# ScalarE issues the weight transfers of the down projection from the third expert on

## What is computed

```
gu = t[tok] @ w_up[e] + b_up[e]                       # 1024 -> 2048
a  = minimum(gu[:, :1024], 7);  u = clip(gu[:, 1024:], -7, 7)
y  = ((u + 1) * a * sigmoid(1.702 * a)) @ w_down[e] + b_down[e]    # 1024 -> 1024
out[tok] += y * gate
```

## Time and profile before

| | us |
|---|---|
| median of 3 runs | 1723.51 |
| the three runs | 1723.09, 1723.51, 1733.51 |
| the profiled execution | 1729.49 |
| its span | 1727.8 |
| TensorE busy in the span | 1650.4 |
| VectorE, ScalarE, GpSimd busy | 522.4, 466.4, 194.3 |

### The profile page before, as it was taken

One profiled execution on the slowest core, in us unless ns is written; L12 is line 12 of the kernel. 1 busy time (PEld: TensorE's weight loads), 2 busy tenths in 40 slices (PEclk: granted clock), 3 DMA queues, 4 the chain that ended last, 5 costly groups with the idle time before them and its releaser, 6 DMA issues.

```text
span 1727.8 us, 44359 instructions
## 1 busy us (share of the span) xinstructions
PE 1650.4 (96%) x19448; PEld 1404.1 (81%) x19448; DVE 522.4 (30%) x1278; ACT 466.4 (27%) x930; POOL 194.3 (11%) x263
## 2 busy tenths in 40 slices
PE   7999999999999999998798999998999998999998
PEld 4899988798777778885445799996799996799996
DVE  6766785655356854000000000000100000000000
ACT  5245655533423432111101121111111111112111
POOL 0022000003331032100000000000000000000000
PEclk9999999999999999899999999999999999999999
DMA  5064232114437319899999999999999999999996
GB/s 227 22 216 119 85 124 100 48 62 134 134 104 268 108 56 386 294 383 400 411 407 401 410 401 402 411 399 389 404 400 407 404 409 389 402 406 398 398 405 241
DMA packets 99340, 499.59 MB, mean 289 GB/s; under 512 B 15198, under 2 KB 32694, under 8 KB 48496
## 3 DMA queue, kind: packets, MB, share of 16 engines
q1 hardware_dynamic: 84288, 458.39, 67.2%
q0 software_dynamic: 14768, 38.71, 8.2%
q10 hardware_dynamic: 144, 0.55, 0.1%
HBM read 485.61 MB, written 22.73 MB: 294 GB/s over the span
## 4 chain that ended last, share of the span: by engine, by line
PE 80%; DMA 11%; DVE 5%; issue 2%; SPq 1%; ACT 1%; POOL 0%; DVEq 0%; POOLq 0%; ACTq 0%
PE bank L1323 22%; PE bank L1321 13%; PE bank L1318 8%; DMA ring<-in_w_exp 8%; PE bank L805 7%; PE bank L705 5%; PE bank L860 5%; PE bank L732 3%; PE bank L1315 2%; PE bank L1124 2%; PE bank L1377 1%; PE bank L873 1%; DMA slab<-in_w_tok 1%; SPq L628 1%; PE bank L894 1%
## 5 line engine op out<-in xcount | busy, mean ns | idle before, releaser
L1323 PE MATMUL bank<-ring,slab 128*32 128x128 f32 x5760 | 644.2, 274 | 0.6 <-issue 0.6
L1321 PE MATMUL bank<-ring,slab 128*32 128x384 f32 x5760 | 636.6, 489 | 3.8 <-DMA ring<-in_w_exp 1.3
L1323 PEld LDWEIGHTS bank<-ring,slab 128*32 128x32 f32 x5760 | 626.0, 110 | 2.0 <-issue 1.3
L2604 DVE TENSOR_SCALAR slab<-bank 128x384 f32<-128x384 f32 (+2 forms) x64 | 33.1, 516 | 922.8 <-PE bank L1323 597.1
L1318 PE MATMUL bank<-ring,slab 128*64 128x256 f32 x2112 | 246.4, 387 | 26.5 <-DMA ring<-in_w_exp 26.0
L1318 PEld LDWEIGHTS bank<-ring,slab 128*64 128x64 f32 x2112 | 149.2, 139 | 113.4 <-DMA ring<-in_w_exp 36.3
L1321 PEld LDWEIGHTS bank<-ring,slab 128*32 128x32 f32 x5760 | 214.0, 109 | 12.2 <-issue 9.9
L1833 ACT ACTIVATE slab<-bank 128x384 f32<-128x384 f32 (+2 forms) x64 | 29.3, 458 | 444.8 <-PE bank L1323 292.8
L805 PE MATMUL bank<-ring_rounded 128*128 128x260 f32 x768 | 147.7, 291 | 0.0
L805 PEld LDWEIGHTS bank<-ring_rounded 128*128 128x128 f32 x768 | 117.8, 188 | 14.0 <-issue 11.9
L2744 POOL DMA_INDIRECT slab<-token_rows,small x31 | 31.1, 1002 | 575.5 <-PE bank L1310 529.9
(11 more groups left out here) (539 smaller groups left out, 2161.0 us busy)
## 6 DMA issues: line engine op xcount, KB each, us to landing
ring<-in_w_exp SPq DMA_DIRECT2D x384, 1024.0 KB
ring<-in_w_blk SPq DMA_DIRECT2D x40, 512.0 KB, 3.6
slab<-in_w_tok SPq DMA_DIRECT2D x4, 1304.0 KB
ring<-in_w SPq DMA_DIRECT2D x8, 512.0 KB, 3.5
ring<-in_w_out SPq DMA_DIRECT2D x2, 2048.0 KB, 14.7
xn<-in_xT SPq DMA_DIRECT2D x4, 520.0 KB
ring<-in_k_cmp SPq DMA_DIRECT2D x32, 64.0 KB, 3.6
ring<-in_k_cmp POOLq DMA_DIRECT2D x32, 64.0 KB, 2.7
```

Of the source, the lines that this page charges most:

```text
L1321: mm(bank[32 * g:32 * g + 32, c, 0:384], rows(32 * g, 32), w[:, 0:384], start=first, stop=last)
L1323: r = mm(bank[96:128, c, P * g:P * (g + 1)], rows(32 * g, 32), w[:, 384:512], start=first and g == 0, stop=last and g == 2)
```

## The change

ScalarE issues the four pieces of the down projection for blocks 2 to 31, at the start of its stream for the block, that is behind `scaled` of the block before. It loads the expert's number into a register of its own for that, and it waits once for `ovf_ready` ahead of the loop. SyncE issues only pieces 0 to 7 of these blocks. Blocks 0 and 1, the path for experts with more tokens than 128 (not taken with these inputs), the semaphores and the places in SBUF stay as they are.

```
@@ SyncE
             def expert(n, after):
                 e = expert_at(n)
-                for c, h in PIECE_ORDER:
+                for c, h in PIECE_ORDER[0:8]:
                     sp.wait_ge(S["half_used"], pieces_used(after, c, h))
                     expert_half(e, c, h)
@@ ScalarE
+            def down_weights(n):
+                e = act.value_load(order_row[0:1, n:n + 1], min_val=0, max_val=NE - 1)
+                for c, h in PIECE_ORDER[8:12]:
+                    act.wait_ge(S["half_used"], pieces_used(n - 1, c, h))
+                    act.dma_start(ring[:, half_of(c, h)], d["w_exp"][bass.ds((e * 6 + c) * P, P), h * HALF:(h + 1) * HALF])\
+                        .then_inc(piece_in[2 * c + h], 16)
...
             block_of(1, role_of(1), CAP[1], CAP[2])
+            act.wait_ge(S["ovf_ready"], 2)
             for n in range(2, NE):
+                down_weights(n)
                 block_of(n, role_of(n), CAP[n], CAP[n + 1] if n + 1 < NE else None)
```

## The result

| | before | after |
|---|---|---|
| median of the runs, us | 1723.51 | 1756.47 |
| lowest to highest | 1723.09 to 1733.51 | 1751.02 to 1759.89 |
| the profiled execution / its span | 1729.49 / 1727.8 | 1756.47 / 1754.8 |
| ratio, with 95% interval | | 1.0167 (1.0140 to 1.0194) |

The changed kernel is slower by 1.67%, 29 us (1.67% of 1724), 24 to 33 by the interval. The ratio is taken over all runs; the two medians alone lie 33.0 us apart, as one of the three runs before is 10 us above the others. The forecast was +24 and 1747.5, within 1727 to 1766.

The account below looks back on a forecast made before the run. Up to block 24's end piece delivery was taken to bound the kernel, afterwards TensorE's own work. Terms of 9 + 14 + 1 gave +24 us, taking the median from 1723.5 to 1747.5 us, range 1727 to 1766.

Parts of the forecast that it names:

- Up to the end of block 24 the time is the delivery of pieces: Whole kernel: piece delivery at 2.73 us each sets the time until block 24 ends, then TensorE's own work, untouched.
- SyncE and ScalarE at nothing: Issuing engines: SyncE's four dropped issues gain nothing; ScalarE's 2.5 us of new work per block fits in 2.94 us idle.
- (a): Ahead of block 2: down pieces issued 11 us later leave the transfer engines idle; +9 us, between 7 and 11.
- (b): Up to block 24's end: two queues alternate, so 5 more pieces are delivered before they are needed; +14 us.
- (c): Long MID blocks: with at most 8 pieces to run ahead, the transfer engines stand idle when all have landed; +1 us.
- MID blocks over 34.2: Sign against the prediction: MID blocks longer than 34.2 us, which no part of its sum holds.
- cross-check by blocks: Sum of expected changes in single blocks 2, 3, 5, 7, 8 and 16: +11 to +19 us.
- delivery account: Counts pieces delivered ahead by block 24's end: lead 5.5 where it was 0, costing 5 x 2.73 = 13.7 us.
- alternation case: Main case: the two hardware queues are served in turn; +24 us, own range 1741 to 1756, chance 0.62.
- Order of issue: Rival: transfers served in the order issued, so only the empty queue ahead of block 2 costs; +9 us, chance 0.15.
- Gaps filled by a second queue: Rival: two queues together move more per us in delivery-bound stretches; 1700 to 1722 us, chance 0.07.
- third rival: Worse than alternation: longer waits lower TensorE's clock in blocks 2, 3, 7, 16 and 24; +10 to +15 more, chance 0.11.

Follow-up runs that it names:

- late-issue run: Kernel before, SyncE issuing all pieces but holding the down pieces of blocks 2 to 31 until the whole block before has used its last piece: 4.7 us over before.
- two complementary sets of blocks: Changed kernel with ScalarE issuing down pieces only for MID blocks behind MID blocks, or only for all other blocks from 2 on: 14.8 and 30.0 us over before.
- 6 us of tiny packets: Kernel before, SyncE issuing all pieces, ScalarE adding the load, waits and four issues per block of 32 bytes a partition into unused columns: 6.2 us over before.
- load and waits alone: Kernel before, SyncE issuing all pieces, ScalarE adding the load of the expert's number and four waits per block, no issue: -1.6 us over before.
- run from block 3 on: Changed kernel, but SyncE issues all 12 pieces of block 2 and ScalarE begins with block 3: 24.3 us over before.
- alternation alone: Against the kernel before, ScalarE issues the next block's down pieces on its own queue as their places come free, within scaled: 15.3 us over before.
- repeated run: The changed kernel unaltered, run again beside the second group of experiments: 29.7 us over before.
- with the full clock: Changed kernel with 12 extra products of 128 columns ahead of three down pieces in blocks 2 to 5, 8, 16 and 24: 37.4 us over before.
- the 3.0 and 5.1 us of blocks 12 and 20: Changed kernel with ScalarE issuing down pieces only for blocks 12 to 14, 20 to 22 and 28 to 30: 5.5 us over before.

## Why the prediction was right

The class, the direction and the main mechanism were right: two queues served in turn, in a stretch bound by the delivery of pieces. That the total came so close owes something to luck. The runs show about 5 us for the term put at 9 and 15 for the one put at 14, and another 9 that appear only with both together and stand in no term.

*What bounds.* "Up to the end of block 24 the time is the delivery of pieces" held: 29.6 of the 30 us in the profile are there at that point. The late-issue run, the two complementary sets of blocks that don't add up, and the 6 us of tiny packets are what a full set of engines would show too.

*SyncE and ScalarE at nothing* held: ScalarE's issues ended 1.2 us before its next work (0.34 us each where 0.41 was taken), and load and waits alone measured -1.6 us (-4.1 to 1.0).

*(a) The dry queue ahead of block 2, +9* was mis-sized. The engines did idle 7.7 us there, but this term measured 4.7 alone (2.2 to 7.2) and 4.5 (28.8 less 24.3) as the difference of the run from block 3 on. Where the other 3 us come back was not found.

*(b) Pieces delivered early, +14* is the part that carried the forecast. The alternation is one to one (4.57 beside 4.19 MB), and alternation alone measured 15.3 (11.7 to 19.1). By the landings in the trace, five up pieces of block 25 had landed when block 24 ended at 1518.8 (the fifth just then; the fourth's landing isn't in the trace and is taken from its place in the queue), the number worked out before. The lengths of single blocks fared less well: at least 28 was said for blocks 2, 3 and 7 (25.7, 30.0, 27.7), about 30 for block 8 (30.4) and 29 for block 16 (30.8). Block 2 is short of it because its up pieces had landed before, so that ScalarE's first piece went alone. And the picture was half right: waits in the down stage were said, up by about 20. They are up by 16, and over half of them are for up pieces of the block itself, in block 3 all of them.

*(c) Idle engines, +1* was too small. The share is 0.94 in block 6 and 0.91 in block 7: 0.06 x 44.1 + 0.09 x 27.7 = 5 us, which the account for (b) had not covered, as it was worked out for block 24 alone. How much of it reaches the end no run tells.

*A term that was missing:* block 9, the first MID block, takes 39 us where it had taken 35.0. The prediction gave MID blocks over 34.2 as a sign that it is wrong, and said that no part of its sum holds them. The sign came true, though the 34.2 was never this block's: the first MID block of each sequence took 35.0, 35.6 and 34.7 before. In the changed kernel its down pieces are issued when up pieces of the block itself are still out, and alternate with those: by the landings in the trace, pieces 5, 6 and 7 of block 9 came at 990.4, 995.4 and 1000.3 us, and 8, 9 and 10 at the same three times. In block 4 the same makes 37.1 of 30.6. In the profile of the repeated run blocks 9, 17 and 25 are longer by 1 to 3 us each.

*The cross-check by blocks* came out lower, at +11 to +19, largely through the windows of blocks 8 and 16: they made block 8 fall by 5, where it fell by 1.5, and block 16 rise by 1, where it rose by 6. Blocks 24 (+4) and 9 (+4) weren't in it. Keeping the delivery account was right.

*The number.* 24 was forecast, 29 measured, with an interval of 24 to 33 that reaches past the case's own range of 18 to 32. The median of 1756.47 lies at the border between the alternation case (1741 to 1756) and the one worse than it (1756 to 1775).

*The rivals.* Order of issue would have given 9 and is refuted by the rates per queue. Gaps filled by a second queue: the rate in bound blocks is 392 to 412 GB/s in blocks 3 to 5, 8, 9, 16 and 24, against 399 to 416 in blocks 4, 5, 8 and 24 before; nothing was filled. Of the third rival the signs came: waits up to 4.0 us, and a clock of 0.82 to 0.94 in more blocks. Its price of +10 to +15 is borne out by no run: with the full clock the kernel was no faster.

The queue round of the Trainium skill ("DMA: Bandwidth & Descriptors", section "Queues, rings and completion order"), by which each DMA engine goes round between the queues that have work, is borne out by block 7's 4.57 and 4.19 MB.

## What to carry to other kernels

When weights stream through a ring of places and the transfers are the limit, one queue in the order of need is itself a resource: a second hardware queue took half of the rate here for whatever stood at its head, needed or not, and both what it carried and what it held up came late. Before moving transfers to another engine, ask when that engine's stream reaches the issue, and what is still outstanding on the first queue at that moment. A wait costs its full length only behind the last stretch that the transfers bound; ahead of it, it is partly given back, as the 3.0 and 5.1 us of blocks 12 and 20 were. And when blocks are compared, cut each window at the first product of the next block: windows 3 us too long made block 16 look half as costly as it was.

## What the runs showed of the hardware that was not expected

Very small transfers aren't free beside a full stream: 120 transfers of 4 KB each (32 bytes a partition) took some 0.6% of the engines' time and came with 6.2 us (2.8 to 9.5), their issues on ScalarE included. Transfers issued first didn't land first: ScalarE's four pieces of block 7 were all issued ahead of SyncE's next one, and landed in turn with SyncE's. And TensorE's clock was granted at 0.82 of full over block 4, so for part of it at 1.2 GHz, where no wait was longer than 3.3 us; keeping TensorE busy with useless products brought it to 1.00 and the kernel no time.
